# Heads 1 to 3 of the mLSTM: key and value blocks computed together with five sevens

## The chip, the cores and the metric

The kernel runs on one core of one Trainium2 chip. The metric is the device time of one execution in microseconds, 1755.02 us as the median of three runs of the kernel before (1754.95 to 1755.1). The engines of the core are TensorE (PE, matrix products into the PSUM banks), VectorE (DVE), ScalarE (ACT), GpSimd (POOL) and SyncE (SP, which issues the loads of the weights).

## The reference

One decoder layer for 256 tokens of width 4096 in float32. The normalised input is multiplied by one wide matrix; its columns feed an mLSTM of four heads and a sparse attention; both are gated, concatenated, projected back, added to the input and normalised.

```python
h = _rmsnorm(x, norm_gain)
proj = h @ w_in
(m_q, m_k, m_v, m_o, m_z, m_i, m_f, a_q, ck, cv, sk, sv, wk, wv, a_gate, a_z) = \
    jnp.split(proj, split_points, axis=-1)
qk = jax.nn.silu(_causal_conv(jnp.concatenate([m_q, m_k], axis=-1), w_conv))
...
h_m = _mlstm(mq, mk, mv, i_pre, f_pre)                # 4 heads: q, k of 256, v of 512 columns
h_m = jax.nn.sigmoid(m_o) * h_m
h_m = h_m * lax.rsqrt(jnp.mean(h_m * h_m, axis=-1, keepdims=True) + RMS_EPS) * gain
y_m = h_m * jax.nn.silu(m_z)
...
mix = jnp.concatenate([y_m, y_a], axis=-1)
x = x + mix @ w_out
return _rmsnorm(x, final_norm_gain)
```

The convolution is causal, per column, four taps wide.

## The kernel before

**Blocks and steps.** The products with `w_in` and `w_out` are cut into blocks of 512 columns. A block has 16 steps (`PAIRS`); each brings 1024 columns of a 128-row weight tile, that is two row tiles of 512, 512 KB, through a ring of four slots (`RING`). SP loads a slot when DVE is through with the raw weights that were in it (L580). ACT copies the raw weights to a rounded high part (`split`, L1170; it waits until PE has used the slot's last contents), DVE subtracts to the low part (`lo`, L1663), and PE multiplies: high by high, high by low and low by high (`passes`, L658 to L660). ACT and DVE issue the parts of step q when PE has ended step q - 4, three steps ahead (`LOOKAHEAD`).

**Eights and sevens.** A plain step takes 2 token tiles x 2 row tiles x 3 matmuls, 12 matmuls of 512 columns (`eight`, L891). Two blocks of equal height can be computed as one "two": where a row pair of both blocks is at hand, the 2 x 2 x 2 products are replaced by seven products of 3 matmuls each (`seven`, L910), 21 matmuls for two steps. A seven needs sums of input tiles, which are made once and kept (`in_s_hi` and, in DRAM, `s_lo_kept`), and four sums of weight tiles, which ACT and DVE make and split for each seven (`split_seven`, L1307; `lo_seven`, L1916: seven DVE instructions at L1935 to L1955). Four of its products go into four shared banks P1, P5, P6, P7, three into the blocks' own banks. At the end of a two DVE adds the shared banks together (`shared_products`, L1969; ACT first copies P1 out at L1333) and adds them to the own banks (`own_products`, L1975); the latter also frees the own bank for the next block (`acc0_free`, `acc1_free`).

**A head of the mLSTM.** Head h has four blocks. The query and key block is a plain stream of eights into acc_a; ACT and DVE scale it into `stage`. The value block is a plain stream into acc_b. At its step 1 PE transposes the key block, DVE runs the four taps of the convolution (`conv`, L2120), ACT the tanh, and at step 13 PE makes the scores. The two gate blocks are one two with six sevens in the order `ORDER_M` (`m_two`, L391): acc_a and acc_b are the own banks. At its step 3 PE makes the numerator. From slot 28 the sums of the sevens follow, in slot 31 `own_products` of the first gate, which frees acc_a, and in slot 0 of the next block that of the second. In the next block, the key block of the following head, DVE and ACT finish the head: `output_gate`, `squares`, a short chain on POOL for the root, `silu_gate`, `head_output`. Heads 0 to 2 run in a loop, head 3 behind it.

**What sets the order.** Each engine issues its instructions in the order in which the program lists them. ACT and DVE have a loop over slots; in slot r they handle the weights of step r + 3 and then the pieces that a table (`piece_map`) gives for slot r. PE has a table of pieces ahead of steps. Semaphores carry the counts between engines.

Of the kernel before, what the change touches and what calls it, by code (L numbers as in the profile page):

```python
# [100 lines left out]
ORDER_M = (6, 7, 8, 0, 9, 1, 10, 2, 11, 3, 12, 4, 13, 5, 14, 15)  # L101
S1, S2, S3, S4 = range(4)
SUM_ORDER, SUMS = (S1, S3, S2, S4), 3
P1, P5, P6, P7 = range(4)
TWO_STEPS = 2 * PAIRS


@dataclass(frozen=True)
class Two:
# [5 lines left out]

    start: Any
    index: Any
    order: tuple
# [5 lines left out]
    def few(self, j):  # L124
        return self.order[j] in SEVEN

    def before(self, j):
        return self.index * len(SEVEN) + sum(c in SEVEN for c in self.order[:j])

    def quads(self):  # L130
        return self.index * len(SEVEN) + len(SEVEN)
# [5 lines left out]
SCORES, NUMERATOR, SHARED_SUMS = 13, 3, 28  # L137
# [47 lines left out]
def hybrid_layer(nc, x, x_cols_first, w_all, final_norm_gain,  # L185
                 consts, early_consts, toe_bias, s_lo_kept, out):
    ctx = ExitStack()
    with ctx:
# [51 lines left out]
        sb("arena", (33 + 56) * KIB // 4 + KIB // 16)  # L240
# [39 lines left out]
        hm = at("hm", Z + 12, TT * BW)[:, :].rearrange("p (a c) -> p a c", a=TT)  # L280
        m_wide = at("m_wide", Z + 32, 8 * P)[:, :].rearrange("p (i m) -> p i m", m=P)
        PADT = T + 3
        conv_in = at("conv_in", Z + 24, 4 * PADT)[:, :].rearrange("p (c t) -> p c t", t=PADT)
        qk = at("qk", Z + 28.25, 4 * T)[:, :].rearrange("p (c t) -> p c t", t=T)
        qk_tanh = flat(ebuf).rearrange("p (c t) -> p c t", t=T)
        qk_hi, qk_lo = [at(n, Z + 32.25 + 4 * i, 4 * T, F32R)[:, :].rearrange(
            "p (c t) -> p c t", t=T) for i, n in enumerate(("qk_hi", "qk_lo"))]
        mv_hi, mv_lo = [at(n, Z + 40.25 + 4 * i, TT * BW, F32R)[:, :].rearrange(
            "p (a c) -> p a c", a=TT) for i, n in enumerate(("mv_hi", "mv_lo"))]
        neg_m = at("neg_m", Z + 16, HEADS_M * T)[:, :].rearrange("p (h t) -> p h t", t=T)  # L290
        neg_m_diag = at("neg_m_diag", Z + 20, HEADS_M * T)[:, :].rearrange(
            "p (h t) -> p h t", t=T)
# [12 lines left out]
        s_raw = forms("s_raw", Z + 40, F32)  # L305
# [6 lines left out]
        kv_s_raw = forms("kv_s_raw", Z + 18, F32)  # L312
        kv_s_hi = sb("in_s_hi", 4 * len(SEVEN) * P, F32R)[:, :].rearrange(
            "p (f c t) -> p f c t", f=4, t=P)
        kv_s_lo = forms("kv_s_lo", Z + 4, F32R)
        kv_t_hi, kv_t_lo = at("kv_t_hi", Z + 48.25, 4 * BW, F32R), at("kv_t_lo", Z + 32, 4 * BW, F32R)
# [6 lines left out]
        m_s_lo = forms("m_s_lo", Z + 28.25, F32R)  # L323
        m_t_hi, m_t_lo = [at(n, Z + 40.25 + 8 * i, 4 * BW, F32R)
                          for i, n in enumerate(("m_t_hi", "m_t_lo"))]
        m_t_raw = at("m_t_raw", Z + 4, 3 * BW)
        m_shared = [[m[:, t, :] for t in range(TT)] for m in (stage, gate_buf)]
# [58 lines left out]
        def kv_two():  # L386

            return Two(KV0, 0, ORDER, ([by, bz], acc[1]), [acc[0][0], acc[0][1], bx, bv],
                       (kv_s_hi, kv_s_lo), (kv_t_hi, kv_t_lo, kv_t_raw))

        def m_two(h):  # L391

            return Two(4 * h * PAIRS + M0, h + 1, ORDER_M, (acc[0], acc[1]), [bx, by, bz, bv],
                       (kv_s_hi, m_s_lo), (m_t_hi, m_t_lo, m_t_raw))

        def out_two(p):

            a, b = [acc[0][0], acc[0][1], bx, bv], [acc[1][0], acc[1][1], by, bz]
            own, shared = (b, a) if p % 2 == 0 else (a, b)
            return Two(TWO0 + p * TWO_STEPS, HEADS_M + 1 + p, ORDER, (own[0:2], own[2:4]), shared,  # L400
                       (s_hi, s_lo), (t_hi, t_lo, t_raw))
# [111 lines left out]
        s_lo_in = sem("s_lo_in")  # L513
        s_raw_done = sem("s_raw_done")
# [138 lines left out]
        def _(pe):  # L653
# [1901 lines left out]
```

## Time and profile before

| | |
|---|---|
| time, median of three runs | 1755.02 us (1754.95 to 1755.1) |
| the profiled execution | 1754.93 us, span 1753.1 us |
| granted PE clock, mean | 0.998 |
| PE busy | 1739.9 us |
| DVE busy | 1259.3 us |
| ACT busy | 922.2 us |
| weights and other bytes | 354.51 MB, mean 202 GB/s |

Times in the rows are microseconds from the span's start. PE's matmuls are pipelined: each shows a duration of about 0.39 us, while one starts about 0.23 us after the other; the pitch of the starts is what counts. A row's bracket names how long the engine had been idle before it, and what ended that.

### The profile page before, as it was taken

To read this page: it belongs to the slowest core of one execution; us is meant where nothing else is said; L and a number is where in the kernel's file an instruction comes from. 1 tells how busy PE (TensorE), PEld (TensorE's weight loads), DVE (VectorE), ACT (ScalarE), POOL (GpSimd) and SP (SyncE) were. 2 spreads that over 40 slices of the span, in tenths; PEclk is the share of its full clock that TensorE was granted. 3 is DMA by queue.
4 is the path that set the end of the run, shared out by engine and by line. 5 is a ranking of instruction groups with operands and counts; after the bars stand their busy time and mean duration, and the time that the engine had idled before them with its cause. 6 is when DMAs were issued, how large, how long until landed. Compare 5 with 4: busy or idle time off the path is not lost.

```text
span 1753.1 us, 23300 instructions
## 1 busy us (share of the span) xinstructions
PE 1739.9 (99%) x8036; PEld 1444.5 (82%) x8036; DVE 1259.3 (72%) x1613; ACT 922.2 (53%) x1271; POOL 19.8 (1%) x33
## 2 busy tenths in 40 slices
PE   9999999999999999999999999999999999999997
PEld 7888888888888888888888888888888888888886
DVE  7557786566675756668856885688568988888876
ACT  7535555455554555545544554455445565564553
POOL 0000000000000000000000000000000000000000
PEclk9999999999999999999999999999999999999999
DMA  9657656545454454555655565556555656666674
GB/s 387 240 177 235 211 201 219 182 161 186 152 184 170 157 188 159 169 197 196 210 190 203 195 213 191 200 196 214 192 197 200 215 182 216 216 217 212 219 261 182
DMA packets 98315, 354.51 MB, mean 202 GB/s; under 512 B 10688, under 2 KB 11200, under 8 KB 97472
## 3 DMA queue, kind: packets, MB, share of 16 engines
q1 hardware_dynamic: 94480, 336.96, 56.2%
q10 hardware_dynamic: 3760, 16.52, 2.6%
q8 instruction: 51, 0.84, 0.2%
q14 instruction: 24, 0.20, 0.0%
HBM read 347.67 MB, written 5.77 MB: 202 GB/s over the span
## 4 chain that ended last, share of the span: by engine, by line
PE 98%; DVE 1%; ACT 0%; issue 0%; DMA 0%; DVEq 0%; POOLq 0%; SPq 0%; POOL 0%; ACTq 0%
PE acc_a L658 14%; PE acc_a L660 14%; PE acc_a L659 14%; PE acc_b L658 13%; PE acc_b L660 13%; PE acc_b L659 13%; PE bank_xy L658 3%; PE bank_xy L659 3%; PE bank_xy L660 3%; PE bank_z L658 1%; PE bank_z L659 1%; PE bank_z L660 1%; PE bank_v L659 1%; PE bank_v L658 1%; PE bank_v L660 1%; PE bank_z L991 1%
## 5 line engine op out<-in xcount | busy, mean ns | idle before, releaser
L1663 DVE TENSOR_TENSOR w_split<-w_raw,w_split 128x1024 fp32r<-128x1024 f32 x519 | 630.7, 1223 | 331.4 <-ACT w_split L1170 328.7
L1170 ACT ACTIVATE w_split<-w_raw 128x1024 fp32r<-128x1024 f32 x518 | 545.0, 1057 | 455.6 <-PE acc_b L660 209.5
L658 PE MATMUL acc_a<-w_split,lhs_hi 128*128 128x512 f32 x1004 | 393.4, 392 | 1.4 <-DVE stage L1975 1.3
L660 PE MATMUL acc_a<-w_split,lhs_lo 128*128 128x512 f32 x1004 | 391.3, 390 | 0.0
L659 PE MATMUL acc_a<-w_split,lhs_hi 128*128 128x512 f32 x1004 | 391.1, 390 | 0.0
L658 PE MATMUL acc_b<-w_split,lhs_hi 128*128 128x512 f32 x938 | 367.3, 392 | 0.0
L660 PE MATMUL acc_b<-w_split,lhs_lo 128*128 128x512 f32 x938 | 365.3, 389 | 0.0
L659 PE MATMUL acc_b<-w_split,lhs_hi 128*128 128x512 f32 x938 | 365.2, 389 | 0.0
L660 PEld LDWEIGHTS acc_a<-w_split,lhs_lo 128*128 128x128 f32 x1004 | 188.4, 188 | 39.9
L658 PEld LDWEIGHTS acc_a<-w_split,lhs_hi 128*128 128x128 f32 x1004 | 188.5, 188 | 39.1 <-DVE stage L1975 2.1
L659 PEld LDWEIGHTS acc_a<-w_split,lhs_hi 128*128 128x128 f32 x1004 | 188.6, 188 | 35.5
L660 PEld LDWEIGHTS acc_b<-w_split,lhs_lo 128*128 128x128 f32 x938 | 176.1, 188 | 37.1
L659 PEld LDWEIGHTS acc_b<-w_split,lhs_hi 128*128 128x128 f32 x938 | 176.2, 188 | 35.1
L658 PEld LDWEIGHTS acc_b<-w_split,lhs_hi 128*128 128x128 f32 x938 | 176.1, 188 | 35.0
L1926 DVE TENSOR_TENSOR w_split<-w_raw,w_split 128x1024 fp32r<-128x1024 f32 x96 | 91.4, 952 | 1.7 <-ACT w_split L1324 1.7
L1314 ACT ACTIVATE w_split<-w_raw 128x1024 fp32r<-128x1024 f32 x48 | 51.0, 1062 | 26.2 <-PE acc_a L660 15.0
L1320 ACT ACTIVATE m_t_hi<-m_t_raw 128x1024 fp32r<-128x1024 f32 x24 | 25.5, 1061 | 54.1 <-PE bank_z L660 47.8
L2050 DVE TENSOR_TENSOR pt_lo<-bank_z,pt_hi 128x512 fp32r<-128x512 f32 (+1 forms) x32 | 17.9, 558 | 49.4 <-ACT pct L1404 49.4
L1402 ACT ACTIVATE pt_hi<-bank_z 128x512 fp32r<-128x512 f32 (+1 forms) x32 | 15.7, 491 | 66.8 <-PE bank_v L993 66.8
L1391 ACT ACTIVATE lg<-lg,nmax 128x256 f32<-128x256 f32 (+1 forms) x64 | 28.7, 449 | 39.3 <-DVE nmax L2028 39.3
L658 PE MATMUL bank_xy<-w_split,lhs_hi 128*128 128x512 f32 x110 | 43.1, 392 | 0.0
L660 PE MATMUL bank_xy<-w_split,lhs_lo 128*128 128x512 f32 x110 | 42.8, 389 | 0.0
(452 smaller groups left out, 1931.8 us busy)
## 6 DMA issues: line engine op xcount, KB each, us to landing
w_raw<-in_w_all SPq DMA_DIRECT2D x614, 512.0 KB
m_s_lo<-s_lo_kept ACTq DMA_DIRECT2D x4, 1536.0 KB, 6.9
wide<-in_x SPq DMA_DIRECT2D x8, 512.0 KB, 10.3
xres<-in_x ACTq DMA_DIRECT2D x8, 512.0 KB, 5.6
out_y<-wide SPq DMA_DIRECT2D x8, 512.0 KB, 3.6
gained_x<-in_x_cols_first SPq DMA_DIRECT2D x6, 512.0 KB, 7.5
toe<-in_toe_bias ACTq DMA_DIRECT2D x4, 512.0 KB, 5.2
gain_f<-in_final_norm_gain ACTq DMA_DIRECT2D x1, 2048.0 KB, 10.0
```

The source lines that it names most:

```text
L658: pe.matmul(dst, a[0], b[0], start=start, stop=False)
L659: pe.matmul(dst, a[0], b[1], start=False, stop=False)
L660: return pe.matmul(dst, a[1], b[0], start=False, stop=stop)
L991: pe.transpose(bz[:, (2 * b + s) * P:(2 * b + s + 1) * P], halves(lg)[:, b, s * P:(s + 1) * P], ident)
L1170: act.activation(w_hi[:, cols], w_raw[:, cols], ACT.Copy).then_inc(hi_done, 1)
L1314: act.activation(w_hi[:, cols], w_raw[:, cols], ACT.Copy).then_inc(hi_done, 1)
L1320: act.activation(sum_hi[:, 0:2 * BW], sum_raw[:, 0:2 * BW], ACT.Copy).then_inc(t13_hi, 1)
L1391: act.activation(halves(lg)[:, b, 0:n], halves(lg)[:, b, 0:n], ACT.Exp, bias=nmax[:, 1 + b:2 + b], accum_out=rsum[:, 1 + b:2 + b])
L1402: act.activation(in_batch(pt_hi, u), transposed_tiles(u), ACT.Copy)
L1663: dve.tensor_tensor(w_lo[:, cols], w_raw[:, cols], w_hi[:, cols].bitcast(F32), ALU.subtract).then_inc(lo_done, 1)
L1926: return dve.tensor_tensor(w_lo[:, cols], w_raw[:, cols], w_hi[:, cols].bitcast(F32), ALU.subtract)
L2050: dve.tensor_tensor(in_batch(pt_lo, u), transposed_tiles(u), in_batch(pt_hi, u).bitcast(F32), ALU.subtract)
```

## The change

The value block of head 0 stays a stream, and the convolution of head 0 lies under it as before. For heads 1 to 3 the key block and the value block become one two (`keys_two`) with five sevens. Its steps are not interleaved: `keys_first(5)` gives two key eights, then five times a seven and two key eights (one behind the last), so that the key block is complete after step 20, and then the eleven value eights. The key's sums are taken in slots 20 and 21, ACT scales the key block in slot 22, PE transposes it ahead of step 23, and the convolution runs under the value eights. Its last tap moves from DVE to ACT. The scores move to step 0 of the gates two, the numerator stays at step 3. The loop of the gates two runs its lookahead on into the key two (`behind`). The pieces that end a head lie in the key two of the next head (`gates_at`), at slots 0, 3, 4 on ACT and 2, 6, 10 on DVE. Several buffers move, the order of the weights in DRAM follows the steps.

```diff
+FEW_V = 5
+def interleaved(order):
+    return tuple((c, h) for c in order for h in range(2))
+
+def keys_first(quads):
+    lead, steps = list(range(quads, PAIRS)), []
+    steps += [(lead.pop(0), 0) for _ in range(max(2, PAIRS - 3 * quads))]
+    for c in range(quads):
+        steps += [(c, 0), (c, 1)]
+        steps += [(lead.pop(0), 0) for _ in range(min(2, len(lead)))]
+    return tuple(steps + [(c, 0) for c in lead] + [(c, 1) for c in range(quads, PAIRS)])
...
-SCORES, NUMERATOR, SHARED_SUMS = 13, 3, 28
+GATES_KEYS, GATES_LAST = (0, 3, 4), (0, 2, 3)
+PRODUCTS_KEYS, PRODUCTS_LAST = (2, 6, 10), (1, 4, 5)
+SCORES, NUMERATOR = 0, 3
+SUMS_GATES, SUMS_KEYS = 28, 20
+CONV_V, CONV_KEYS = 1, 23
...
+        def keys_two(h):
+            return Two(4 * h * PAIRS + (M0 + TWO_STEPS), 2 * h + 2, per_head * h + 2 * len(SEVEN),
+                       FEW_V, keys_first(FEW_V), (acc[0], acc[1]), [bx, by, bz, bv],
+                       (kv_s_hi, m_s_lo), (m_t_hi, m_t_lo, m_t_raw))
...  PE, in eight
-                    if free is not None:
-                        pe.wait_ge(*free[t])
+                    if own_free is not None and w.opens(r, h, t):
+                        wait_for([own_free[h][t]])
...  PE
+            def own_blocks(b):
+                return [((acc0_free, b + i), (acc1_free, b + i)) for i in range(2)]
+            def gates(h):
+                two(gates_two(h), (), ((hm_done, h + 1), (s_lo_in, h * 16 + 16)),
+                    own_blocks(4 * h + B_MLSTM), True, head_pieces(h))
+            def keys(h):
+                w = keys_two(h)
+                two(w, ((seven_free, w.index),), (), own_blocks(4 * h + (B_MLSTM + 2)), True,
+                    {CONV_KEYS: [lambda: conv_columns(h + 1, ((seven_free, w.index + 1),
+                                                              (keys_scaled, h + 1)))]})
...
             with pe.Fori(0, HEADS_M - 1) as h:
-                head(h)
-                stream(4 * h + (B_MLSTM + 3), 0)
-            head(HEADS_M - 1)
+                gates(h)
+                keys(h)
+            gates(HEADS_M - 1)
...  ACT
+                def last_tap(i):
+                    for c in (2 * i, 2 * i + 1):
+                        last = act.activation(qk[:, c, :], tiles((bv, bx)[i][:, :])[:, c % 2, :],
+                                              ACT.Copy, scale=conv_tap(h, c, 3))
+                    last.then_inc(tap_done, 1)
+                def key_scale():
+                    act.wait_ge(acc0_free, b + 4)
+                    act.wait_ge(acc1_free, b + 4)
                     for t in range(TT):
+                        last = act.activation(m_shared[0][t], m_shared[0][t], ACT.Copy,
+                                              scale=rstd[:, t:t + 1])
+                    last.then_inc(keys_scaled, 1)
...  DVE (ACT's two_stream likewise)
-            def two_stream(w, pieces):
+            def two_stream(w, pieces, behind=None):
                 for r in range(LOOKAHEAD, TWO_STEPS + LOOKAHEAD):
-                    j, h = divmod(r, 2)
-                    if r >= TWO_STEPS or not w.few(j):
-                        lo(w.start + r, r % RING)
-                    elif h == 0:
-                        lo_seven(w, j)
+                    u, i = (w, r) if r < TWO_STEPS or behind is None else (behind, r - TWO_STEPS)
+                    if i >= TWO_STEPS or not u.few(i):
+                        lo(u.start + i, i % RING)
+                    elif u.steps[i][1] == 0:
+                        lo_seven(u, i)
                     for piece in pieces.get(r - LOOKAHEAD, ()):
                         piece()
...  DVE
+                def sums_at(w, c, last):
+                    return (*[(c + part // 2, lambda part=part: shared_products(w, m_shared, part))
+                              for part in range(4)], (last, lambda: own_sums(w, 0)))
+                two_pieces = ((SCORES, scores), (SCORES + 1, values_lo), (SCORES + 2, scores_lo),
+                              (NUMERATOR + 1, lambda: normalise(0)),
+                              (NUMERATOR + 1, lambda: normalise(1)),
+                              *sums_at(gates_two(h), SUMS_GATES, SUMS_GATES + 3))
+            def gates(h, late=(), behind=None):
+                two_stream(gates_two(h), piece_map(*head_pieces(h)[0], *late), behind)
+            def keys(h):
+                _, _, gates_at, sums_at, own_sums = head_pieces(h)
+                two_stream(keys_two(h), piece_map(
+                    *gates_at(*PRODUCTS_KEYS), *sums_at(keys_two(h), SUMS_KEYS, CONV_KEYS - 2),
+                    *head_pieces(h + 1)[1](CONV_KEYS)))
+                own_sums(keys_two(h), 1)
```

## Rows read from the trace of the kernel before

**Rows 1.** The page's busy times: engine, busy us, share of the span, instructions.

```profile
PE 1739.9 (99%) x8036; PEld 1444.5 (82%) x8036; DVE 1259.3 (72%) x1613; ACT 922.2 (53%) x1271; POOL 19.8 (1%) x33
```

**Rows 2.** The waits of PE: who waited for whom, us in total, times, longest.

```profile
PE acc_a L658 <- DVE stage L1975: 1.3, 4, 0.4
```

**Rows 3.** PE's timeline (start, duration, instruction): a seven, an eight, the next seven.

```profile
818.70 0.39 PE L658 MATMUL bank_xy<-w_split,lhs_hi 128*128 128x512 f32 x1
...
823.46 0.39 PE L658 MATMUL acc_a<-w_split,lhs_hi 128*128 128x512 f32 x1
...
828.89 0.39 PE L658 MATMUL bank_xy<-w_split,lhs_hi 128*128 128x512 f32 x1
```

**Rows 4.** DVE's timeline at the end of head 0's gates two.

```profile
869.49 0.68 DVE L1969 TENSOR_TENSOR stage<-bank_v,gate_buf 128x512 f32<-128x512 f32 x1
870.21 0.69 DVE L1969 TENSOR_TENSOR gate_buf<-bank_xy,stage 128x512 f32<-128x512 f32 x1
870.99 1.23 DVE L1663 TENSOR_TENSOR w_split<-w_raw,w_split 128x1024 fp32r<-128x1024 f32 x1
...
873.71 1.23 DVE L1663 TENSOR_TENSOR w_split<-w_raw,w_split 128x1024 fp32r<-128x1024 f32 x1 [0.89 <-ACT w_split L1170]
874.85 1.28 DVE L1975 TENSOR_TENSOR stage<-acc_a,stage 128x512 f32<-128x512 f32 x2
```

**Rows 5.** PE's timeline there: the gates' last matmul, the next block's first.

```profile
874.91 0.39 PE L660 MATMUL acc_b<-w_split,lhs_lo 128*128 128x512 f32 x1
875.59 0.50 PE L658 MATMUL acc_a<-w_split,lhs_hi 128*128 128x512 f32 x1 [0.29 <-DVE stage L1975]
```

**Rows 6.** DVE's timeline over one seven's preparation, and the start of a later one.

```profile
831.56 1.23 DVE L1935 TENSOR_TENSOR m_t_raw<-w_raw 128x1024 f32<-128x1024 f32 x1
...
835.01 1.23 DVE L1945 TENSOR_TENSOR m_t_lo<-m_t_raw,m_t_hi 128x1024 fp32r<-128x1024 f32 x1 [0.36 <-ACT m_t_hi L1320]
836.27 0.69 DVE L1950 TENSOR_TENSOR m_t_raw<-w_raw,m_t_raw 128x512 f32<-128x512 f32 x1
...
838.09 1.23 DVE L1955 TENSOR_TENSOR m_t_lo<-m_t_raw,m_t_hi 128x1024 fp32r<-128x1024 f32 x1 [0.53 <-ACT m_t_hi L1327]
839.23 2.38 DVE L1663 TENSOR_TENSOR w_split<-w_raw,w_split 128x1024 fp32r<-128x1024 f32 x2
...
852.81 1.23 DVE L1935 TENSOR_TENSOR m_t_raw<-w_raw 128x1024 f32<-128x1024 f32 x1 [0.99 <-DMA w_raw<-in_w_all]
```

**Rows 7.** ACT's timeline at the end of head 0's gates two.

```profile
872.61 1.06 ACT L1170 ACTIVATE w_split<-w_raw 128x1024 fp32r<-128x1024 f32 x1 [1.66 <-PE acc_a L660]
875.41 1.06 ACT L1170 ACTIVATE w_split<-w_raw 128x1024 fp32r<-128x1024 f32 x1 [1.74 <-PE acc_b L660]
```

**Rows 8.** ACT's timeline: its last split for the seven of rows 6.

```profile
836.99 1.06 ACT L1327 ACTIVATE m_t_hi<-m_t_raw 128x1024 fp32r<-128x1024 f32 x1 [1.50 <-DVE m_t_raw L1950]
```

**Rows 9.** Groups by line: head_output (instructions, busy us, mean ns, idle before).

```profile
L2191 DVE SCALAR_TENSOR_TENSOR wide<-hm,hr,gate_buf 128x512 f32 (+1 forms) x8 | 5.6, 746 | 0.0
```

**Rows 10.** ACT's timeline in the next block: first square, then the tanh.

```profile
885.05 0.61 ACT L1516 ACTIVATE ebuf<-hm 128x512 f32<-128x512 f32 x1
...
888.02 1.34 ACT L1526 ACTIVATE ebuf<-gate_buf,rstd_half 128x512 f32<-128x512 f32 x2 [0.16 <-POOL hr L2410]
```

**Rows 11.** PE's timeline: the first matmul of head 0's scores, the eight behind.

```profile
779.72 0.28 PE L658 MATMUL bank_xy<-qk_hi 128*128 128x256 f32 x1
...
781.05 0.45 PE L658 MATMUL acc_b<-w_split,lhs_hi 128*128 128x512 f32 x1
```

**Rows 12.** DVE's timeline: the low part of the scores.

```profile
788.98 0.55 DVE L2153 TENSOR_TENSOR sw_lo<-sw,sw_hi 128x384 fp32r<-128x384 f32 x1
```

**Rows 13.** DMA issues: queue, count, KB each, median us to landing.

```profile
m_s_lo<-s_lo_kept ACTq DMA_DIRECT2D x4, 1536.0 KB, 6.9
```

**Rows 14.** Stretches at the end: length, busy us by engine, PE clock, DMA, GB/s.

```profile
1742.00:1743.00 1.00, 0.93 (x5) 0.43 (x3) 0.28 (x2) 0.00 (x0) 0.00 (x0) 1.00 1.02 418
...
1746.00:1747.00 1.00, 0.00 (x0) 0.00 (x0) 1.00 (x3) 0.00 (x0) 0.00 (x0) 0.68 0.81 332
```

**Rows 15.** PE's timeline: the warm-up matmuls at the start.

```profile
1.45 3.78 PE L707 MATMUL bank_v<-warm 128*128 128x512 f32 x8 [1.45 <-DVE warm L1711]
```

More of the change, by code:

```diff
@@ L117 @@
     index: Any
-    order: tuple
+    base: Any
+    quads: int
+    steps: tuple
     own: tuple
@@ L122, with few, before, within @@
     t: tuple
[L124 to L131, printed above, removed]
-GAINS = 8
-SCORES, NUMERATOR, SHARED_SUMS = 13, 3, 28
+    def few(self, r):
+        return self.steps[r][0] < self.quads
+    def before(self, r):
+        return self.base + self.within(r)
+    def within(self, r):
+        return sum(self.few(i) for i in range(0, r)) // 2
+    def after(self):
+        return self.base + self.quads
+    def touches(self, r, h, t):
+        c, block = self.steps[r]
+        if self.few(r):
+            return block == 0 and (h, t) != (1, 1)
+        return block == h
+    def opens(self, r, h, t):
+        return not any(self.touches(i, h, t) for i in range(r))
+    def closes(self, r, h, t):
+        return not any(self.touches(i, h, t) for i in range(r + 1, len(self.steps)))
+    def last(self, h):
+        return max(r for r in range(len(self.steps)) if self.touches(r, h, 0))
+GAINS = 8
+GATES_KEYS, GATES_LAST = (0, 3, 4), (0, 2, 3)
[3 more added lines that the diff above has]
+CONV_V, CONV_KEYS = 1, 23
 RESIDUAL = 12
@@ L1315, in split_seven @@
                 act.wait_ge(t13_raw, n + 1)
-                if sums_free is not None and w.order[j] == SEVEN[0]:
+                if sums_free is not None and w.within(r) == 0:
                     act.wait_ge(*sums_free)
@@ L1549, in _ @@
-                act.wait_ge(mz_done, h + 1)
-                take(4 * h + (B_MLSTM + 3), 0, stage[:, 0, :])
+                gates(h, behind=keys_two(h))
+                keys(h)
             def input_sums_hi(f):
@@ L2210, in head, with conv_at @@
-            def head(h, late={}):
-                b = 4 * h + B_MLSTM
-                of_values, of_two, of_gates = head_pieces(h)
-                for c, more in late.items():
-                    of_two.setdefault(c, []).extend(more)
-                stream(b, of_values)
-                dve.wait_ge(tr_done, h + (T_MQK + 1))
-                take(b, 1, stage[:, 1, :])
-                two_stream(m_two(h), of_two)
-                return of_gates
+                def conv_at(c):
+                    return ((c, conv_inputs), *[(c + 1 + j, lambda j=j: conv(j)) for j in range(3)],
+                            (c + 5, qk_gate), (c + 7, qk_lo_part))
@@ L2221, in _ @@
+            stream(B_MLSTM, piece_map(*head_pieces(0)[1](CONV_V)))
+            dve.wait_ge(pe_used, B_MLSTM * PAIRS + (PAIRS + extra))
+            dve.tensor_copy(m_shared[1][1], acc[1][1][:, :]).then_inc(acc1_free, 1)
             with dve.Fori(0, HEADS_M - 1) as h:
                 chain.enter(h, HEAD_LINKS)
-                stream(4 * h + (B_MLSTM + 3), head(h))
-                dve.wait_ge(mo_e, h + 1)
-                take(4 * h + (B_MLSTM + 3), 0, stage[:, 1, :])
+                gates(h, behind=keys_two(h))
+                keys(h)
@@ L2239, in input_sum_lo @@
                     last.then_inc(s_lo_done, 1)
-            late = head(HEADS_M - 1, {MIX_TAIL + c: [lambda c=c: mix_lo(c)] for c in range(MIX_M)})
+            gates(HEADS_M - 1, [(MIX_TAIL + c, lambda c=c: mix_lo(c)) for c in range(MIX_M)])
+            late = piece_map(*head_pieces(HEADS_M - 1)[2](*PRODUCTS_LAST))
             for i, f in enumerate(SUM_ORDER):
@@ L2299, in own_sums @@
                 dve.wait_ge(seven_free, two.index + 1)
-                dve.wait_ge(pe_used, two.start + TWO_STEPS - 1 + h)
+                dve.wait_ge(pe_used, two.start + two.last(h) + 1)
                 for t in range(TT):
```

341 lines of the change are left out of this document (183 added, 158 removed).

## The prediction

> **What bounds the kernel now.** I read the page's busy line first: PE is busy 1739.9 of 1753.1 us, no other engine above 72% [rows 1]. Then the waits of PE: in the whole execution its largest group of waits inside the stream is four short ones on the same addition, 1.3 us together [rows 2]. So PE is the bound almost everywhere. A matmul that is taken out is worth its full pitch, and a new wait of PE costs its full length. The change is therefore a sum of matmuls removed and PE waits added, and the second half of the sum is decided by the order in which DVE and ACT issue.
>
> The run that the rows come from took 1754.93 us (span 1753.1 and 1.8 around it), 0.1 below the median of 1755.02. I add to 1754.93.
>
> **Matmuls removed.** A seven and the two eights behind it take 828.89 - 818.70 = 10.19 us on PE, and the seven alone 823.46 - 818.70 = 4.76 [rows 3]. A seven is 7 products of 3 matmuls, two eights are 24 matmuls, so 45 matmuls take 10.19 us (0.226 each; an eight of 12 takes 2.72). The change makes 5 sevens out of 10 eights in each of three heads: 3 matmuls less in each of 15, again 45. Saved: **10.2 us**, hard to miss, as nothing else on PE is added (the transposes, scores and numerators are the same instructions at other steps).
>
> **The seam between a gates two and the key two behind it.** Before, DVE ended the low part of the last-but-one stage at 870.99 + 1.14 = 872.13 (1.14 is the pitch of such instructions, 873.71 to 874.85), did one more low part, and issued at 874.85 the additions `own_products` that free acc_a [rows 4]. PE's last gate matmul started at 874.91 and the next block's first at 875.59, 0.74 after the additions had started [rows 5]: 0.45 us lost, one of the four waits.
>
> After the change the lookahead of the gates' loop runs into the key two (`behind`). `keys_first(5)` puts only two key eights ahead of the first seven, and the lookahead is 3, so at the last turn of the loop DVE issues the whole of `lo_seven` for step 2, and only then the piece of slot 31, which is `own_products` of the gates' first half. The first key eight opens acc_a again and waits for exactly this addition. How long is `lo_seven`? From its first instruction at 831.56 to the instruction behind its last at 839.23 are 7.67 us, with 0.36 in it that came from the seven before [rows 6]; that one is absent here, so 7.3. Its end can't be drawn forward: ACT may overwrite the slot of the last gate stage only when PE is through with it (875.41 [rows 7]), and its last split starts when DVE has made the fourth sum (836.99, straight after 836.27 + 0.69 [rows 6, 8]). From 872.13 the additions start at 879.4 and PE at 880.2 in place of 875.59: 4.6 us more per head, **+13.8** for three. Bounds: 0, if the order worked out above were not the order issued; not below, because the addition can't come before the last gate eight but one as it does now; 16.8 if the weights of that seven come 1 us late each time, as once before (0.99 ahead of 852.81 [rows 6]). I take 13.8, since every duration has its row.
>
> **The squeeze in the first half of the key two.** Count from PE's new start there. DVE has 4.9 us of new pieces between sevens: two additions 1.28, two gate products of 1.14, and `head_output`, two of 0.746 that overlap (about 1.35) [rows 4, 9]. ACT gets two squares, a wait for POOL and two tanh: 888.02 - 885.05 = 2.97 from the first square to the tanh, and 1.34 for the tanh [rows 10].
> Step 1 ends at 5.4; ACT starts 0.2 later and DVE 1.1 after that (872.61, 873.71 [rows 4, 7]), so the low part of step 5 is through at 7.9, the output gate at 9.0, and the second `lo_seven` starts. Its fourth sum ends 5.0 later (836.27 + 0.69 - 831.56 less 0.4), at 14.0; ACT's last split of it ends at 15.1, squares and POOL bring the tanh to 18.1, its end to 19.4, the split of step 8 to 20.4, DVE's low part to 21.6. PE wants step 8 after two eights, a seven, two eights and a seven: 20.4. Wait: 1.3.
> Then DVE has two low parts, the silu product and 7.3 of `lo_seven`: end 31.1; PE starts that seven at 21.7 + 5.4 = 27.1 and wants its last sums after 15 matmuls, 3.4 later: 30.5. Wait: 0.6. The next turn has `head_output` in place of the silu product and gives 0.6 again; after it DVE catches up. Sum 2.5 per head, **+7.5**. Bounds: 0, because before the change DVE is ahead there (it ends the sums of a seven at 838.09 + 1.23, 0.2 after that seven began at about 839.1, where they are wanted 3.4 later [rows 3, 6]); 14.7, if all 4.9 us land on PE. I take the count, which is half.
>
> **The convolution under the value eights.** Its transposes stand before step 23. Counted from the start of step 21: DVE's low part ends at 2.4, two additions at a pitch of 0.72 (869.49, 870.21 [rows 4]) end at 3.9, `own_products` at 5.2; ACT then scales the key block, two of 512 columns (1.34, nearest row the tanh [rows 10]): 6.6. PE is there after two eights, at 5.4. Wait 1.2 per head, **+3.6**; bounds 0 and 2.7 (DVE late by half a `lo_seven`). The taps behind it are covered by eight more eights (21.8 us).
>
> **The scores at step 0.** They take 781.05 - 779.72 = 1.33 as before [rows 11], but now the numerator follows after three eights, not ten steps and more. Step 2 starts; ACT 0.2, DVE 1.1 later, 1.14 for the low part, 0.55 for the scores' low part [rows 4, 12]: 3.0 against an eight of 2.72. Wait 0.3, four heads: **+1.2**; bounds 0 and 4 (one low part more ahead of it).
>
> **Costed at nothing.** The copy of `s_lo_kept` back into m_s_lo is issued behind the scores and lands after 6.9 us [rows 13]; six eights and a numerator (over 16 us) pass before the first seven reads it. Without that cover it would cost at most 6.9 a head. The last taps on ACT (four short ones a head) replace four DVE ones and stand where ACT has a split per eight. Weight bytes and their order of use are the same in number; the moved buffers cost nothing by themselves.
>
> **Sum:** -10.2 + 13.8 + 7.5 + 3.6 + 1.2 = +15.9; 1754.9 + 15.9 = 1770.8, say **1771 us**.
>
> **The clock of PE.** At the end of the trace PE's last matmul lies in 1742 to 1743 with the granted clock at 1.00; in 1746 to 1747 it is 0.68, on its way from 2.4 to 1.2 GHz, with nothing for PE in between [rows 14]. The new idle time at the seam is about 875.3 to 880.2, as long as that. At the lower level eight warm-up matmuls took 3.78 us, 0.47 each [rows 15]. The Trainium skill, "TensorE: Matmul & The Clock Gate", Part 1, states that an idle PE is put to half its clock and earns it back by sustained activity; the trace agrees with the first half [rows 14]. By that rule each seam would lose some 8 x (0.47 - 0.226) = 2.0 us more.
>
> **The rivals.**
> (a) The seam alone: DVE and ACT keep up in the key two and at the convolution. For it: DVE's lead of 3 us in a seven [rows 6]; against it: ACT's wait for POOL stands ahead of a split. 1754.9 - 10.2 + 13.8 = 1758.5, with small waits up to 1763.
> (b) The clock falls at the three seams. 2.0 each, less the 1.3 that the slower start gives DVE and ACT back: +2 to +6, 1773 to 1777, and 1782 with the squeeze at its worst. For it the end of the trace [rows 14]; against it, that the idle time only just reaches that length.
> (c) Faster. One mechanism: at the seam the additions that free acc_a are through before DVE is held by the seven, so PE waits 0.45 as now. Then the 10.2 stands against the small waits: 1744.7 without any, 1751 with half of them. It decides where the seam costs less than 3.4 us a head (10.2 / 3), which needs a `lo_seven` of under 6 us; its rows have no slack for that [rows 6], so only a wrong reading of the order leads there.
> (d) The change doesn't remove what it says: if fewer sevens ran, 1771 would rise by 0.68 for each; the steps are written out, so I give it nothing of its own.
>
> **From the cases to the numbers.** My sum (1763 to 1779) 0.55; (a) 0.16; (b) 0.15; (c) 0.11; the remaining 0.03 beyond 1782. What a measurement here can tell from no change is 0.2%, 3.5 us: 1751.5 to 1758.5. (c) gives faster 0.11; half of (a) gives same 0.08; the rest is slower, 0.81. The range leaves out (c) and the far end: 1755 to 1781.
>
> **What would show it.** In the changed profile: matmuls fewer by 45; one PE wait of about 5 us per key two, on `own_products` into stage, with the DVE rows ahead of it those of a seven; waits of about 1.3 before the transposes, released by ACT's scaling; waits under 1.5 on the low parts near the second seven. Total PE idle time of about 26 us more. The prediction is wrong if the wait at the seam is under 3 us, or if the waits within the key two exceed the one at the seam.

## The result, and the profile after

The changed kernel took **1781.05 us** (median of 4 runs, 1779.69 to 1782.97) beside 1755.06 for the kernel before in the same session: a ratio of 1.0148, 95% interval [1.0136, 1.0161]. It is 26.0 us slower. The forecast was 1771 us with a range of 1755 to 1781: the direction was right, the size was 10 us short, and the time lies just past the range's upper end. The profiled execution has a span of 1780.1 us, 27.0 more than before. One of the nine executions of the kernel with the gate products later (below) took 4530.11 us at a granted clock of 1.00; it is left out of that kernel's ratio, and no trace shows what held it.

First the page's line of busy times of the changed kernel (engine, busy us, share of the span, instructions), to read against [rows 1]:

```profile
PE 1742.2 (98%) x7991; PEld 1440.8 (81%) x7991; DVE 1325.9 (74%) x1694; ACT 951.2 (53%) x1324; POOL 18.1 (1%) x33
```

PE has 8036 - 7991 = 45 matmuls fewer, as forecast. They should make it 10.2 us less busy, and it is 2.3 us more busy. So the new time isn't idle time alone: some matmuls have become slower.

The waits of PE in the changed kernel (who waited for whom, us in total, times, longest), to read against [rows 2]:

```profile
PE acc_a L721 <- DVE stage L2087: 14.7, 4, 4.8
PE bank_v L763 <- ACT stage L1612: 4.7, 3, 1.6
PE acc_a L721 <- DVE w_split L1775: 3.2, 3, 1.1
PE acc_a L721 <- DVE m_t_lo L2067: 1.9, 6, 0.4
PE bank_xy L721 <- DVE sw_lo L2262: 1.6, 4, 0.7
```

These are the places that the prediction named, in the same number: three seams (the fourth of the first group is the old short one), three transposes, three waits for the low part of step 8, six near the second seven and the one behind it, four numerators.

**The seam.** DVE's timeline at the end of head 0's gates two (start, duration, instruction, idle before), to read against [rows 4]:

```profile
872.97 1.22 DVE L2047 TENSOR_TENSOR m_t_raw<-w_raw 128x1024 f32<-128x1024 f32 x1
...
879.03 1.23 DVE L2067 TENSOR_TENSOR m_t_lo<-m_t_raw,m_t_hi 128x1024 fp32r<-128x1024 f32 x1 [0.52 <-ACT m_t_hi L1410]
880.17 1.28 DVE L2087 TENSOR_TENSOR stage<-acc_a,stage 128x512 f32<-128x512 f32 x2
```

The additions that free acc_a (880.17) stand behind the whole of the seven's preparation, which takes 880.17 - 872.97 = 7.2 us where 7.3 was reckoned. PE's timeline at the same place, to read against [rows 5]:

```profile
875.75 0.39 PE L723 MATMUL acc_b<-w_split,lhs_lo 128*128 128x512 f32 x1
880.91 0.79 PE L721 MATMUL acc_a<-w_split,lhs_hi 128*128 128x512 f32 x1 [4.78 <-DVE stage L2087]
881.50 0.63 PE L722 MATMUL acc_a<-w_split,lhs_hi 128*128 128x512 f32 x1
...
886.62 0.49 PE L722 MATMUL acc_a<-w_split,lhs_hi 128*128 128x512 f32 x1
886.96 0.39 PE L723 MATMUL acc_a<-w_split,lhs_lo 128*128 128x512 f32 x1
...
1065.60 0.79 PE L721 MATMUL acc_a<-w_split,lhs_hi 128*128 128x512 f32 x1 [4.78 <-DVE stage L2087]
```

The last of these lines is the same place in head 1. Look at the starts. Before the wait and again behind 886.96 they are 0.23 apart; from 881.50 to 886.62 twelve pitches take 5.12, 0.427 each. The stretches of the changed kernel there (length, busy us of PE, weight loads, DVE, ACT and POOL, granted clock, DMA share, GB/s) say why:

```profile
879.00:880.00 1.00, 0.00 (x0) 0.00 (x0) 0.97 (x1) 0.00 (x0) 0.00 (x0) 1.00 0.87 254
880.00:881.00 1.00, 0.09 (x1) 0.09 (x1) 1.00 (x3) 0.00 (x0) 0.00 (x0) 0.50 1.08 434
881.00:886.00 5.00, 5.00 (x12) 3.94 (x13) 1.65 (x3) 1.33 (x2) 0.00 (x0) 0.50 0.18 72
887.00:888.00 1.00, 1.00 (x6) 0.83 (x5) 0.39 (x1) 0.57 (x1) 0.00 (x0) 1.00 0.00 0
```

PE's granted clock is 0.50, 1.2 GHz, when the wait ends, and is back at 1.00, 2.4 GHz, from 887. The same happens at the other two seams (12 slow matmuls each, 13 here).

**The squeeze behind it.** ACT in the first half of the key two, to read against [rows 10]:

```profile
886.51 1.06 ACT L1253 ACTIVATE w_split<-w_raw 128x1024 fp32r<-128x1024 f32 x1 [3.63 <-PE acc_a L723]
...
897.79 1.06 ACT L1410 ACTIVATE m_t_hi<-m_t_raw 128x1024 fp32r<-128x1024 f32 x1 [1.95 <-DVE m_t_raw L2062]
...
901.86 1.34 ACT L1623 ACTIVATE stage<-m_gate,rstd_half 128x512 f32<-128x512 f32 x2 [1.78 <-POOL hr L2531]
903.10 1.99 ACT L1253 ACTIVATE w_split<-w_raw 128x1024 fp32r<-128x1024 f32 x2
```

and PE, at the first matmuls that this and the later groups of waits hold up in head 0:

```profile
905.46 0.50 PE L721 MATMUL acc_a<-w_split,lhs_hi 128*128 128x512 f32 x1 [1.09 <-DVE w_split L1775]
905.80 0.40 PE L722 MATMUL acc_a<-w_split,lhs_hi 128*128 128x512 f32 x1
...
947.34 0.65 PE L763 MATMUL bank_v<-c,stage 128*128 128x128 f32 x4 [1.54 <-ACT stage L1612]
...
983.00 0.49 PE L721 MATMUL bank_xy<-mv_hi,sw_hi 128*128 128x512 f32 x1 [0.51 <-DVE sw_lo L2262]
```

Squares, POOL's step and the tanh stand between the last split of the second seven (897.79) and the splits behind it (903.10), as counted.

**Where the 26 us come from.** A wait is best taken from the starts of PE's matmuls: start of the one that waited, less start of the one before, less a full pitch of 0.227. In head 0's seam that is 880.91 - 875.75 - 0.23 = 4.93. The list says 4.78 there, since it counts idle time from the modelled end of the matmul before, 0.39 after its start. A slow matmul is taken in the same way, its pitch less 0.227. The rows of all heads, summed in this way:

| term | forecast us | measured us |
|---|---|---|
| 45 matmuls less | -10.2 | -10.2 |
| seams, less the four short waits of before | +13.8 | +13.5 |
| step 8 (3 waits) and the sevens' low parts (6) | +7.5 | 3.7 + 2.8 = +6.5 |
| transposes (3) | +3.6 | +5.2 |
| numerators (4) | +1.2 | +2.2 |
| waits together | +26.1 | +27.4 |
| 37 matmuls at half the clock, beyond their full pitch | 0 | +7.8 |
| second pitch behind a wait (0.34 for 0.23, 905.46 to 905.80) | 0 | +1.2 |
| sum | +15.9 | +26.2 |

The measured sum is 0.8 below the 27.0 between the two spans; these rows don't say where that is. The waits were forecast to 5%. What the sum left out is the clock.

### The profile page after: what moved, and what is told of

Its sections match the earlier page's. It is cut to its first block, busy times and chain, and to the rows that moved or that the text cites. A ratio compares the mean times of both kernels' runs of the same rounds, so it can differ in the third digit from the quotient of the medians.

```text
span 1780.1 us, 23476 instructions
## 1 busy us (share of the span) xinstructions
PE 1742.2 (98%) x7991; PEld 1440.8 (81%) x7991; DVE 1325.9 (74%) x1694; ACT 951.2 (53%) x1324; POOL 18.1 (1%) x33
## 4 chain that ended last, share of the span: by engine, by line
PE 67%; issue 31%; DVE 1%; DMA 1%; ACT 0%; POOL 0%; POOLq 0%; DVEq 0%; ACTq 0%; SPq 0%
PE acc_a L721 9%; PE acc_a L723 9%; PE acc_a L722 9%; PE acc_b L721 8%; PE acc_b L723 8%; PE acc_b L722 8%; PE bank_xy L721 2%; PE bank_xy L722 2%; PE bank_xy L723 2%; PE bank_z L721 1%; PE bank_z L722 1%; PE bank_z L723 1%; PE bank_v L722 1%; PE bank_v L721 1%; PE bank_v L723 1%
## 5 line engine op out<-in xcount | busy, mean ns | idle before, releaser
L1253 ACT ACTIVATE w_split<-w_raw 128x1024 fp32r<-128x1024 f32 x488 | 510.4, 1055 | 361.3 <-PE acc_b L723 158.5
L721 PE MATMUL acc_a<-w_split,lhs_hi 128*128 128x512 f32 x959 | 380.0, 396 | 18.1 <-DVE stage L2087 14.7
L722 PE MATMUL acc_a<-w_split,lhs_hi 128*128 128x512 f32 x959 | 376.7, 393 | 0.0
L723 PE MATMUL acc_a<-w_split,lhs_lo 128*128 128x512 f32 x959 | 376.6, 393 | 0.0
L721 PE MATMUL acc_b<-w_split,lhs_hi 128*128 128x512 f32 x878 | 343.7, 391 | 0.0
L723 PE MATMUL acc_b<-w_split,lhs_lo 128*128 128x512 f32 x878 | 342.0, 389 | 0.0
L722 PE MATMUL acc_b<-w_split,lhs_hi 128*128 128x512 f32 x878 | 341.9, 389 | 0.0
L721 PEld LDWEIGHTS acc_a<-w_split,lhs_hi 128*128 128x128 f32 x959 | 182.1, 190 | 56.3 <-DVE stage L2087 15.6
L722 PEld LDWEIGHTS acc_a<-w_split,lhs_hi 128*128 128x128 f32 x959 | 182.2, 190 | 34.2
L721 PEld LDWEIGHTS acc_b<-w_split,lhs_hi 128*128 128x128 f32 x878 | 164.9, 188 | 33.0
L722 PEld LDWEIGHTS acc_b<-w_split,lhs_hi 128*128 128x128 f32 x878 | 164.9, 188 | 32.8
L1403 ACT ACTIVATE m_t_hi<-m_t_raw 128x1024 fp32r<-128x1024 f32 x39 | 41.3, 1060 | 84.8 <-PE bank_z L723 47.8
L1397 ACT ACTIVATE w_split<-w_raw 128x1024 fp32r<-128x1024 f32 x63 | 66.9, 1061 | 35.8 <-PE acc_a L723 19.5
L1410 ACT ACTIVATE m_t_hi<-m_t_raw 128x1024 fp32r<-128x1024 f32 x39 | 41.3, 1060 | 62.0 <-DVE m_t_raw L2062 62.0
L2067 DVE TENSOR_TENSOR m_t_lo<-m_t_raw,m_t_hi 128x1024 fp32r<-128x1024 f32 x39 | 47.8, 1226 | 19.4 <-ACT m_t_hi L1410 19.4
L2047 DVE TENSOR_TENSOR m_t_raw<-w_raw 128x1024 f32<-128x1024 f32 x39 | 47.7, 1222 | 10.4 <-DMA w_raw<-in_w_all 6.3
L2057 DVE TENSOR_TENSOR m_t_lo<-m_t_raw,m_t_hi 128x1024 fp32r<-128x1024 f32 x39 | 47.6, 1221 | 8.4 <-ACT m_t_hi L1403 8.4
```

The lines of the kernel that those rows point to most:

```text
L721: pe.matmul(dst, a[0], b[0], start=start, stop=False)
L722: pe.matmul(dst, a[0], b[1], start=False, stop=False)
L723: return pe.matmul(dst, a[1], b[0], start=False, stop=stop)
L1253: act.activation(w_hi[:, cols], w_raw[:, cols], ACT.Copy).then_inc(hi_done, 1)
L1397: act.activation(w_hi[:, cols], w_raw[:, cols], ACT.Copy).then_inc(hi_done, 1)
L1403: act.activation(sum_hi[:, 0:2 * BW], sum_raw[:, 0:2 * BW], ACT.Copy).then_inc(t13_hi, 1)
```

## The experiments

Each kernel was timed in turn with the kernel before on the same chip. The edits are to the changed kernel unless another is named.

**The seam's order.** The gates' own addition one slot earlier, so that it isn't behind the seven in DVE's queue:

```diff
-                              *sums_at(gates_two(h), SUMS_GATES, SUMS_GATES + 3))
+                              *sums_at(gates_two(h), SUMS_GATES, SUMS_GATES + 2))
```

> The additions that free acc_a at the end of the gates two move from slot 31 to slot 30 on DVE, so ahead of the first seven of the key two; nothing else. Theory (the order on DVE makes the seam, and the idle time there lets the PE clock fall): the wait of 4.8 us and the matmuls at 0.43 us behind it go in all three heads, 1781 - 3 x (4.5 + 2.9) = 1759; since DVE no longer has the first seven ready early, the wait ahead of step 8 may grow by up to 2 us a head, so 1759 to 1765. Rival (DVE is simply short of time in the key two, with five sevens and the end of a head in it): the wait only moves to the low parts behind, and the time stays at 1775 or more.

Measured: 1767.37 us, ratio 1.0070 [1.0053, 1.0087]. The long wait at the seam is gone; the first waits of PE are now

```profile
PE acc_a L721 <- DVE w_split L1775: 8.1, 4, 2.6
PE bank_v L763 <- ACT stage L1612: 6.3, 3, 2.5
```

The seam and its slow matmuls cost 13.5 + 7.8 = 21.3. By the medians 13.7 came back, by the spans of the two profiled executions 16.1. The two waits above took 4.9 and 1.6 more, and two new falls of the clock 3.3; the waits on the sevens' low parts, three in place of six, gave back another 1.1. PE of this kernel behind the wait of step 8, in the three heads:

```profile
899.08 0.50 PE L721 MATMUL acc_a<-w_split,lhs_hi 128*128 128x512 f32 x1 [2.64 <-DVE w_split L1775]
...
900.24 0.63 PE L722 MATMUL acc_a<-w_split,lhs_hi 128*128 128x512 f32 x1
...
1079.03 0.50 PE L721 MATMUL acc_a<-w_split,lhs_hi 128*128 128x512 f32 x1 [2.62 <-DVE w_split L1775]
1079.36 0.40 PE L722 MATMUL acc_a<-w_split,lhs_hi 128*128 128x512 f32 x1
...
1258.31 0.79 PE L721 MATMUL acc_a<-w_split,lhs_hi 128*128 128x512 f32 x1 [2.62 <-DVE w_split L1775]
```

So the order at the seam, with the fall of the clock that it brings, is the largest single cause, shown. The time is 2.4 us above the theory's range: the wait of step 8 grew by 1.5 a head, as the theory allowed, but the falls of the clock behind it and the longer transposes' wait were not in it.

**The clock by itself.** 20 matmuls that compute nothing used go into bank_v while PE waits at the seam; DVE and ACT are left as they are:

```diff
                 w = keys_two(h)
+                pe.wait_ge(seven_free, w.index)
+                for i in range(20):
+                    pe.matmul(bv[:, :], kv_s_hi[:, 0, 0, :],
+                              lhs_hi[:, 0:2, :].rearrange("p k t -> p (k t)"), start=True, stop=True)
                 two(w, ((seven_free, w.index),), (),
```

> Adds work: PE issues 20 matmuls into the idle bank P7 ahead of each key two (60 in all, results overwritten), about 4.5 us that lie inside the 4.8 us wait at the seam. Theory (the low clock behind the seam is its second price): the granted clock stays at 2.4 GHz, the first key eight runs at 0.227 us a matmul in place of 0.43, and the time falls by 3 x 2.9 to about 1772 although work is added. Rival (the missing time is not the clock's): 1781 or a little more.

Measured: 1776.99 us, ratio 1.0127 [1.0110, 1.0143]; span 1774.0, 6.1 less than the changed kernel's. PE at the seam of head 0:

```profile
876.75 0.39 PE L723 MATMUL acc_b<-w_split,lhs_lo 128*128 128x512 f32 x1
876.98 4.70 PE L1172 MATMUL bank_v<-lhs_hi,in_s_hi 128*128 128x512 f32 x20
881.93 0.50 PE L721 MATMUL acc_a<-w_split,lhs_hi 128*128 128x512 f32 x1 [0.25 <-DVE stage L2091]
882.26 0.39 PE L722 MATMUL acc_a<-w_split,lhs_hi 128*128 128x512 f32 x1
882.49 0.39 PE L723 MATMUL acc_a<-w_split,lhs_lo 128*128 128x512 f32 x1
...
1064.00 0.50 PE L721 MATMUL acc_a<-w_split,lhs_hi 128*128 128x512 f32 x1 [0.25 <-DVE stage L2091]
```

The last gate matmul and the first key eight are 5.18 us apart, as in the changed kernel (5.16), but the key eight now runs at 0.23 a matmul, and behind the kernel's first 20 us no slow matmul is left in the trace. So the fall of the clock is a cost of its own, beside the wait: 4.1 us by the medians, 6.1 by the spans, where the rows of the changed kernel give 7.8 for its slow matmuls.

The traces say where the difference lies. From the first key eight of head 0 to that of head 1 it is 1065.60 - 880.91 = 184.69 us in the changed kernel and 1064.00 - 881.93 = 182.07 here: 2.6 less, where head 0's slow matmuls cost 2.8. The next head gives 2.5, and from the last key two's start to the block behind the last gates two it is 2.0, with a transposes' wait that is 0.4 longer: 7.2 in all. The spans show 1.0 less, since this execution came to the first seam 1.0 later (876.75 for 875.75), ahead of anything that was edited. The medians show less still: the three other executions have a granted clock of 0.997, the profiled one 0.998, and where they lost it no trace shows. The theory's 1772 is 5 us below the median.

**Four sevens in place of five**, `FEW_V = 4`: the first seven then comes later, and the seam is free of it.

> FEW_V = 4 in place of 5: four key eights stand ahead of the first seven, so no seven lies in the gates' lookahead. Theory (order at the seam): 36 matmuls saved in place of 45 (8.2 us), the seam costs 0.45 a head as before the change, the clock does not fall; waits left: 1.6 a head before the transposes, about 0.4 at each numerator, under 1 a head on low parts: 1755 - 8.2 + 4.7 + 1.6 + 0 to 3 = 1753 to 1756. Rival (DVE short of time): one seven less a head takes 3 x 7 us from DVE, the time falls by at most the waits that this relieves, to 1768 or more.

Measured: 1755.83 us, ratio 1.0003 [0.9994, 1.0013]. The seams' wait is 1.3 us in four, as before the change, and the clock holds. With 36 matmuls less it gains 8.2, and by starts it loses 5.0 to the transposes (4.5 listed), 2.6 to the numerators (1.9 listed) and 0.4 to the second pitches: no change.

**The key block's additions earlier** (all five in slot 20, the scaling on ACT in slot 21):

```diff
-                    *gates_at(*PRODUCTS_KEYS), *sums_at(keys_two(h), SUMS_KEYS, CONV_KEYS - 2),
+                    *gates_at(*PRODUCTS_KEYS),
+                    *[(SUMS_KEYS, lambda part=part: shared_products(keys_two(h), m_shared, part))
+                      for part in range(4)], (SUMS_KEYS, lambda: own_sums(keys_two(h), 0)),
...
-... (SUMS_KEYS, key_product), (CONV_KEYS - 1, key_scale)
+... (SUMS_KEYS, key_product), (SUMS_KEYS + 1, key_scale)
```

> All five additions of the key block in slot 20 (before: slots 20 and 21 with the low part of step 24 between them), ACT's scaling one slot earlier, in slot 21. Theory (the transposes wait because the chain is cut by one slot of the weight stream): the wait of 1.5 us before the transposes goes, 3 x 1.7 = 5 us: 1776. Rival (the chain is as long without the low part in it): no change, 1781, with the wait now on a low part.

Measured: 1778.73 us, ratio 1.0137 [1.0120, 1.0153]. The transposes' wait falls from 4.7 to 2.2 listed, most of it in one head (a third wait, 0.3, is listed under "issue"):

```profile
PE bank_v L763 <- ACT stage L1612: 2.2, 2, 1.7
```

The spans of the two profiled executions differ by 3.6: by starts 2.2 are the transposes', and 1.6 are shorter slow stretches behind the seams (6.3 for 7.8), which the edit doesn't aim at. The order of the additions explains half of the transposes' wait. The 1.7 that stays is head 2's, and there the rows show another cause. ACT of this kernel ahead of the scaling:

```profile
1302.33 1.06 ACT L1253 ACTIVATE w_split<-w_raw 128x1024 fp32r<-128x1024 f32 x1 [0.52 <-DMA w_raw<-in_w_all]
1304.43 1.06 ACT L1253 ACTIVATE w_split<-w_raw 128x1024 fp32r<-128x1024 f32 x1 [1.04 <-DMA w_raw<-in_w_all]
...
1310.95 1.33 ACT L1612 ACTIVATE stage<-stage,rstd 128x512 f32<-128x512 f32 x2 [3.67 <-DVE stage L2087]
```

Its splits wait 0.52 + 1.04 us for weights, DVE's low parts wait for the splits, and the additions stand behind those. In head 0, where the same two splits have 0.61, PE isn't held by ACT there at all.

**The gate products later**, on top of the seam's order:

```diff
-GATES_KEYS, GATES_LAST = (0, 3, 4), (0, 2, 3)
-PRODUCTS_KEYS, PRODUCTS_LAST = (2, 6, 10), (1, 4, 5)
+GATES_KEYS, GATES_LAST = (0, 5, 7), (0, 2, 3)
+PRODUCTS_KEYS, PRODUCTS_LAST = (2, 9, 14), (1, 4, 5)
```

> The shared additions ahead of the seven (as in the run with the gates' own addition in slot 30) and, in the first half of the key two, the squares, the tanh and the gate products of ACT and POOL spread over later steps (0, 5, 7 and 2, 9, 14 in place of 0, 3, 4 and 2, 6, 10). That run left a step-8 wait of 2.6 us and one fall of PE's clock behind it. Theory: the step-8 wait and the fall are made by the squares, POOL's step and the tanh, which stand ahead of the splits on ACT: with them later the 2.6 goes, PE waits on the low part of step 8 under 1 us in each head, the clock stays at 1.00 through the key two, and the time is 1760 to 1764 (1767.4 less three times 1.5 to 2.5). Rival: DVE is late there by itself (its seven and the new additions): the wait stays at 2 us or more and the time within 2 us of 1767.

Measured: 1759.68 us, ratio 1.0025 [1.0014, 1.0036]: 7.7 below the seam's order alone (in which the clock fell twice, at 900.24 and 1258.31, not once). Its waits of PE:

```profile
PE bank_v L763 <- ACT stage L1612: 5.7, 3, 2.1
...
PE acc_a L721 <- DVE w_split L1775: 0.2, 1, 0.2
```

The 8.1 us of the low part of step 8 are 0.2. So ACT's squares, POOL's step and the tanh ahead of the splits made that wait, as the theory has it; the clock falls once, behind the longest wait that is left (2.09 us, the transposes of head 1). The time came out slightly below the theory's range. It is a median over executions that differ: from 1755.01 us at a granted clock of 0.998 to 1763.67 at 0.994, in between longer as the clock is lower.

**The tanh alone later** in the changed kernel, `GATES_KEYS = (0, 3, 5)`:

> The after kernel with one number changed: the second half of the gate activation (the tanh that waits for POOL) at step 5 of the key two in place of step 4. Theory: the wait ahead of step 8 (1.1 us per head, 3.2 in all) comes from ACT's wait for POOL ahead of the split: it goes, the seam stays as it is with its fall of the clock, 1776 to 1779. Rival: step 8 is late because DVE is: the wait stays over 0.8 us each and the time within 1.5 us of 1781.

Measured: 1782.71 us, ratio 1.0151 [1.0134, 1.0168], no different from the changed kernel. The wait did go, and came back under other names:

```profile
PE bank_v L763 <- ACT stage L1612: 5.9, 3, 2.4
PE acc_a L721 <- DVE m_t_lo L2067: 2.5, 6, 0.5
...
PE bank_xy L721 <- DVE w_split L2038: 1.3, 3, 0.4
PE acc_a L721 <- DVE w_split L1775: 0.2, 1, 0.2
```

3.0 less at step 8, and 1.3 + 0.6 + 1.2 = 3.1 more behind it. DVE of this kernel shows the way for the first two:

```profile
905.02 1.23 DVE L1775 TENSOR_TENSOR w_split<-w_raw,w_split 128x1024 fp32r<-128x1024 f32 x1 [2.54 <-ACT w_split L1253]
...
913.37 1.23 DVE L2067 TENSOR_TENSOR m_t_lo<-m_t_raw,m_t_hi 128x1024 fp32r<-128x1024 f32 x1 [0.53 <-ACT m_t_hi L1410]
```

The tanh now stands ahead of the split of step 9, and DVE is held there instead. From 905.02 to its last low part for the next seven (913.37; 913.66 in the changed kernel) it has no idle time but that 0.53, so one split earlier at step 8 brings that low part 0.3 earlier and no more, and PE waits for it. Of the 1.2 at the transposes 0.9 is in head 2, where ACT's splits waited 1.17 and 1.16 us for weights, and a fourth fall of the clock stands behind it, with five slow matmuls (1.1 us) that the list of waits doesn't show:

```profile
1316.66 0.90 PE L763 MATMUL bank_v<-c,stage 128*128 128x128 f32 x4 [2.41 <-ACT stage L1612]
```

By starts, from the first key eight to the next numerator, heads 0 and 1 are 0.5 and 0.1 us shorter than in the changed kernel and head 2 is 2.2 longer. The theory was right on what makes the wait, wrong on what it is worth. In the run above, with the tanh at step 7 and the gate products at steps 9 and 14, the gain stayed.

**The scores' parts earlier**:

```diff
-                two_pieces = ((SCORES, scores), (SCORES + 1, values_lo), (SCORES + 2, scores_lo),
+                two_pieces = ((SCORES, scores), (SCORES + 1, scores_lo), (SCORES + 1, values_lo),
...
-... (SCORES + 1, sw_hi_part),
+... (SCORES, sw_hi_part),
```

> The after kernel with the scores' own parts one slot earlier (the split of the scores on ACT in slot 0, their low part on DVE ahead of the values' low part in slot 1). Theory: PE's waits on the low part of the scores (1.6 us in four) go and nothing else moves: 1778.5 to 1780. Rival: the low part of step 1 to 2 is then late instead, or PE waits the same: 1781 or more.

Measured: 1783.71 us, ratio 1.0166 [1.0149, 1.0183]; the rival's side. The 1.6 us on the scores' low part became

```profile
PE bank_xy L721 <- DVE mv_lo L2288: 2.1, 2, 1.1
```

on the values' low part. The numerator wants both; the order of the two decides only which is last.

**All of it together**, five sevens kept (the seam's order, the gate products later, the key additions earlier, the scores' parts earlier):

> All four reorderings together with five sevens kept: the gates' own addition in slot 30, the gate products spread, the key additions all in slot 20 with the scaling in slot 21, the scores' low part one slot earlier. Theory: of the after kernel's idle time on PE about 5 of 25 us are left and the clock does not fall, so the 45 matmuls that the change removes (10.2 us) show: 1747 to 1752, faster than before. Rival: each piece of work that is moved delays the next, the waits come back elsewhere (over 12 us in sum): 1758 or more.

Measured: 1753.52 us, ratio 0.9990 [0.9981, 1.0000], 27.5 us below the changed kernel, and 1.5 above the theory's range. The trace has no slow matmul behind the start. Its waits:

```profile
PE bank_xy L721 <- DVE mv_lo L2288: 2.3, 2, 1.2
PE bank_v L763 <- ACT stage L1612: 2.2, 3, 0.8
PE acc_a L721 <- DVE m_t_lo L2067: 1.8, 6, 0.4
```

6.3 us are left in eleven waits, and behind eight of them (all but the transposes) the second pitch.

**The same without the scores' edit**:

> The all-together kernel (1753.5) without its reordering of the scores: five sevens, the gates' own addition in slot 30, the gate products spread, the key additions in slot 20. Theory, after the run of the scores alone: DVE has both low parts to make before the numerator whichever comes first, so the wait only changes its name; without that edit PE waits some 1.8 us in four on the scores' low part in place of 2.3 on the values', and the time is 1752 to 1754, ratio to before 0.998 to 0.9995. Rival: the edit was worth something in this order: 1755 or more.

Measured: 1753.47 us, ratio 0.9988 [0.9979, 0.9997]: the scores' order is worth nothing, as the theory had it.

**Four sevens with the key additions earlier**:

> Four sevens in place of five (36 matmuls less than before in place of 45, about 8.2 us; the run with four alone took 1755.8, with 4.5 us of waits ahead of the transposes) and all key additions in slot 20. Theory: the transposes' wait shrinks from 1.5 to under 0.8 a head, the rest stays: 1752 to 1754. Rival: DVE is late there for another reason than the order (its seven before), and the wait stays: 1755.5 or more.

Measured: 1751.64 us, ratio 0.9979 [0.9970, 0.9988], the fastest of all, with nearly nothing left of the waits at the transposes:

```profile
PE bank_v L763 <- issue: 0.5, 3, 0.2
```

The time is 0.4 under the theory's range. The order of the additions takes nearly the whole of this wait away with four sevens, where with five it took half. This version beats the kernel before by 3.9 us, out of 8.2 that its 36 matmuls are worth.

## Why the prediction was right in sign and wrong in size

**Matmuls removed** (-10.2): right; 45 are gone, and the pitch is the same 0.227 where the clock holds.

**The seam** (+13.8): right, in order and in length; 13.5 by the starts. Moving the one addition made the wait go.

**The squeeze** (+7.5): right in place and near in size, 6.5. The count had 1.3, 0.6 and 0.6 per head; the rows have 1.2, 0.5 and 0.5. That the tanh ahead of the split makes the first of them is shown by the two runs that moved it; the other two are DVE's: in the changed kernel it goes from 904.18 to 926 through two sevens, the silu product and `head_output` with no idle time but 0.53 twice.

**The transposes** (+3.6): right in place, 5.2 in size, 1.7 a head for 1.2. In head 0 step 21 starts at 947.34 - 1.70 less two eights of 2.72, that is 940.20; DVE's additions end at 945.45 and ACT's scaling at 946.87, 5.25 and 6.67 later, where 5.2 and 6.6 were counted. What the count left out is the last hop: PE starts 0.47 after ACT has ended.

**The numerators** (+1.2): 2.2. By starts they are 0.40, 0.67, 0.81 and 0.32 in heads 0 to 3. In heads 0 and 3 the 0.3 is about right. In heads 1 and 2 DVE comes late to the values' low part (979.86, 1.41 us long in head 1) and goes from it straight to the low part of step 2 (981.19), which the count had starting 1.1 after ACT's split.

**The step that failed is the clock of PE.** The prediction had the mechanism as rival (b), gave it 0.15, and priced it at 2.0 a seam (eight slow matmuls, the number of the warm-up) less 1.3 that the slower start would give DVE and ACT back. It had put PE's idle time at "as long as that" and took this as an argument against the fall. The clock fell at every seam of every kernel that kept the 4.78 us wait: four traces with three seams each, without one exception; in the changed kernel 12 or 13 matmuls a seam were slow, and they cost 7.8 us, 2.6 a seam; and nearly nothing was given back. ACT's splits wait for PE, so a slow PE makes them late too: the first one behind the seam of head 0 is released by PE and starts 5.60 us after the first key eight (886.51), 3.13 after it where the clock held (885.06 in the kernel with the matmuls in the gap), and PE waits 1.09 us ahead of step 8 in both. All listed waits behind the seams are 11.4 us here and 11.9 there. The Trainium skill, "TensorE: Matmul & The Clock Gate", Part 1, says that an idle PE drops to half its clock and has to earn it back with sustained activity; these traces agree with both halves (0.50 from 880 to 886, 1.00 from 887). The kernel with the matmuls in the gap shows that the cost is the clock's and not the wait's. The signs of being wrong that the prediction named were both about waits, and neither came (4.78 at the seam; 6.5 + 5.2 us within the key twos against 13.5 at the seams): they couldn't show this miss.

The remaining 2.5 us are 1.3 in the waits and 1.2 in the pitch behind each wait, which the sum had at nothing.

One thing is not settled. ACT's splits wait for weights 20.5 + 9.0 us in the changed kernel, 11.3 + 3.1 before. In four traces with five sevens one head has a split that waited 1.02 to 1.17 us for weights shortly ahead of the transposes, and PE's wait at the transposes is 0.6 to 1.4 us longer there than in the other two heads (2.53 with the seam's order, 1.67 with the key additions earlier, 2.41 with the tanh later, 2.20 with the scores' parts earlier). With four sevens splits waited 2.35 and 1.75 there without that. No run moved the loads, so what these waits cost elsewhere is open.

## What to carry to other kernels

Where one engine is the bound to 99%, a new wait on it has three prices: its own length, the pitch behind it, and, behind some waits (here all of 4.78 us and some of 2.1 to 2.6), a stretch at half the clock that can cost half as much again; look first at what stands in the same queue ahead of the instruction that ends the wait, because moving one addition one slot was worth 14 us here. When a wait is taken away and the time stays, compare the sum of all waits, not the one: work that is late is waited for at the next place, until it is moved behind the point where its engine has slack.
A cut in the bound engine's work (10.2 us here) is worth having only as far as the helpers keep up: four fifths of the cut with one reordering (1751.6) gave a little more than the whole with three (1753.5).

## What the runs showed of the hardware that was not expected

The same wait doesn't always bring the same clock. Behind three waits of 2.62 to 2.64 us, in one trace and at the same place of three heads, the clock was down at once (1258.31), after three matmuls (900.24), and not at all (1079.36). A wait of 2.53 us at the transposes of that kernel had none behind it; one of 2.41 in the kernel with the tanh later had five slow matmuls, one of 2.09 in the kernel with the gate products later eight. Behind the 4.78 us waits the slow stretch was 6 to 13 matmuls long; the shortest is in the kernel with the key additions earlier, in head 1:

```profile
1064.07 0.80 PE L721 MATMUL acc_a<-w_split,lhs_hi 128*128 128x512 f32 x1 [4.78 <-DVE stage L2087]
...
1066.79 0.45 PE L721 MATMUL acc_a<-w_split,lhs_hi 128*128 128x512 f32 x1
```

So in these runs the length of the wait alone doesn't decide; what else does was not tested.
